# Group norms of SSD and retention: squares and sums on Pool, one ones product per group, retention's heads in two PSUM banks

## The reference

```python
z, xbc, dt_raw, rq, rk, rv, rg = _split(h @ w_in, AB_SIZES)
...
y = (y + xs * d_skip[:, None]).reshape(bsz, l, SSD_D_INNER) * jax.nn.silu(z)
y = group_rms(y, SSD_GROUPS) * ssd_norm
...
r, ret_s = retention_scan(q, k, v, ret_s)
r = jax.nn.silu(rg) * group_rms(r.reshape(bsz, l, RET_V), RET_HEADS)
return jnp.concatenate([y, r], axis=-1) @ w_out, conv_buf, ssm_h, ret_s
```

## Time and profile before

| what | value |
|---|---|
| device time, three runs | 1846.28, 1851.96, 1851.95 us (median 1851.95) |
| the profiled execution: its device time, its span from first to last instruction | 1851.53 us, 1849.6 us |
| busy share of the span: PE, DVE, ACT, POOL | 93%, 68%, 46%, 14% |
| mean granted TensorE clock (share of full speed) | 0.971 |
| the first product of r0, the start of the output projection's matmuls (us from the span's start) | 554.32, 633.96 |

### The profile page before, as it was taken

The page is one execution under the profiler, slowest core; times in us unless marked ns, Lnnn a source line. Parts: engine busy times, 40 slices in busy tenths (PEclk is TensorE's granted clock), DMA queues, the critical chain, the costliest instruction groups (busy, mean ns, idle before and its releaser), DMA issues.

```text
span 1849.6 us, 34017 instructions
## 1 busy us (share of the span) xinstructions
PE 1725.2 (93%) x13610; PEld 1631.4 (88%) x13610; DVE 1255.1 (68%) x2260; ACT 848.8 (46%) x1156; POOL 251.6 (14%) x353
## 2 busy tenths in 40 slices
PE   7999989898997899989999999999997898999998
PEld 7999989887885689887999999999886787799997
DVE  5765677686676654594677767776656678477764
ACT  5433455364336533333455555445444642344443
POOL 1001100200111112120200121002311122020011
PEclk9999989999999898999999999999999998999999
DMA  8665745445576576686698798889834578578884
GB/s 229 182 171 163 212 133 153 131 122 158 170 241 193 179 249 181 212 290 244 172 254 244 227 258 250 264 249 277 244 98 153 175 241 313 188 205 247 268 272 147
DMA packets 470522, 386.58 MB, mean 209 GB/s; under 512 B 15401, under 2 KB 436549, under 8 KB 470341
## 3 DMA queue, kind: packets, MB, share of 16 engines
q1 hardware_dynamic: 409904, 254.87, 47.4%
q0 software_dynamic: 27200, 97.11, 15.5%
q10 hardware_dynamic: 33280, 32.65, 5.2%
HBM read 346.12 MB, written 38.66 MB: 208 GB/s over the span
## 4 chain that ended last, share of the span: by engine, by line
PE 61%; DVE 18%; ACT 14%; issue 6%; DMA 2%; POOL 0%; ACTq 0%; DVEq 0%; SPq 0%; POOLq 0%
PE psum L264 16%; PE psum L265 16%; PE psum L266 16%; DVE wlo L218 6%; ACT whi L212 5%; DVE kc L2300 2%; ACT late L1819 2%; DVE late L1828 2%; PE psum L596 1%; PE psum L2376 1%; PE psum L485 1%; PE psum L2471 1%; PE psum L831 1%; PE psum L1627 1%; PE psum L2419 1%
## 5 line engine op out<-in xcount | busy, mean ns | idle before, releaser
L218 DVE TENSOR_TENSOR wlo<-raw,whi 128x2048 fp32r<-128x2048 f32 (+2 forms) x261 | 552.9, 2119 | 267.5 <-ACT whi L212 266.8
L264 PE MATMUL psum<-xnh,whi 128*128 128x264 f32 x2328 | 675.3, 290 | 12.3 <-DVE ht L851 6.9
L265 PE MATMUL psum<-xnl,whi 128*128 128x264 f32 x2328 | 666.5, 286 | 0.0
L266 PE MATMUL psum<-xnh,wlo 128*128 128x264 f32 x2328 | 665.5, 286 | 0.0
L212 ACT ACTIVATE whi<-raw 128x2048 fp32r<-128x2048 f32 (+2 forms) x261 | 460.8, 1767 | 116.9 <-DMA raw<-in_w_xkv 45.6
L264 PEld LDWEIGHTS psum<-xnh,whi 128*128 128x128 f32 x2328 | 445.8, 191 | 26.2 <-issue 25.2
L265 PEld LDWEIGHTS psum<-xnl,whi 128*128 128x128 f32 x2328 | 445.9, 192 | 1.1
L266 PEld LDWEIGHTS psum<-xnh,wlo 128*128 128x128 f32 x2328 | 443.4, 190 | 0.0
L264 PE MATMUL psum<-Hh,whi 128*128 128x264 f32 x704 | 201.6, 286 | 1.6 <-DVE late L1828 1.6
L266 PE MATMUL psum<-Hh,wlo 128*128 128x264 f32 x704 | 200.6, 285 | 0.0
L265 PE MATMUL psum<-Hl,whi 128*128 128x264 f32 x704 | 200.3, 285 | 0.0
(11 more groups left out here) (589 smaller groups left out, 2906.7 us busy)
## 6 DMA issues: line engine op xcount, KB each, us to landing
raw<-in_w_ffn_in SPq DMA_DIRECT2D x176, 512.0 KB, 5.2
raw<-in_w_in_ab SPq DMA_DIRECT2D x88, 512.0 KB, 4.7
raw<-in_w_ffn_out SPq DMA_DIRECT2D x64, 384.0 KB, 4.6
out<-late ACTq DMA_DIRECT2D x48, 512.0 KB, 5.2
raw<-in_w_ffn_out SPq DMA_DIRECT2D x64, 320.0 KB, 3.5
sb<-in_state_ret POOLq DMA_DIRECT2D x32, 512.0 KB, 5.1
raw<-in_w_out_ab SPq DMA_DIRECT2D x32, 512.0 KB, 5.1
kc<-in_cache_mem_k POOLq DMA_DIRECT2D x32, 512.0 KB, 6.4
```

Source lines behind the costliest of these rows:

```text
L218: nc.vector.tensor_tensor(wlo[:, c % SLOTS, 0:m], raw[:, c % SLOTS, 0:m], whi[:, c % SLOTS, 0:m].bitcast(F32), ALU.subtract).then_inc(lo_d ...
L264: e.matmul(out, a, hi[:, kk, 0:S.cols], start=first, stop=False)
L265: e.matmul(out, a, lo[:, kk, 0:S.cols], start=False, stop=False)
L266: m = e.matmul(out, b, hi[:, kk, 0:S.cols], start=False, stop=final)
```

## The change

Pool squares the four tiles of a group and adds them up in the place where the group's root will stand (`Squares`); PE then runs one ones product for the group (`SumRoot`), followed by the same root and reciprocal. The statistics r0, y0, r1, y1 and so on are taken in this order. Pool's squares are put between its loads of retention states; the gate's multiplication that overwrites a tile of `vf` waits for the group's squares. The SSD groups' applications move: y2 from the hooks of chunk 5 to those of chunk 6, y3 from chunk 6 to chunk 7. Even and odd heads of the sample retention use banks 5 and 7, so a head waits for the copy of the head before the last.

```diff
+        class Squares(Stage):
...
+            def pool(S, e):
+                if S.before:
+                    S.before(e)
+                acc = S.out[:, 0, 0:S.n]
+                for t in range(S.g):
+                    v = S.src[:, t, 0:S.n]
+                    link(e, "pool", e.tensor_tensor(sq[:, t % 2, 0:S.n] if t else acc, v, v, ALU.mult))
+                    if t:
+                        ins = e.tensor_tensor(acc, acc, sq[:, t % 2, 0:S.n], ALU.add)
+                        if t < S.g - 1:
+                            link(e, "pool", ins)
+                ins.then_inc(sq_ready, 1)
+
+        class SumRoot(Stage):
...
+            def pe(S, e):
+                if S.q.g0 > 0:
+                    e.wait_ge(sd_done, S.q.g0)
+                e.wait_ge(sq_ready, S.q.q0 + 1)
+                e.matmul(psum[:, SSB, 0:S.q.n], ones[:, :], S.q.out[:, 0, 0:S.q.n], start=True, stop=True).then_inc(ss_done, 1)
+
+            def act(S, e):
+                e.wait_ge(ss_done, S.q.q0 + 1)
+                nc.scalar.activation(S.q.out[:, 0, 0:S.q.n], psum[:, SSB, 0:S.q.n], ACT.Sqrt, scale=1.0 / (S.q.g * P), bias=eps).then_inc(sd_done, 1)
...
-            part_of = lambda h: slice((h % 2) * 256, (h % 2) * 256 + 256)
+            bank_of = lambda h: 5 + 2 * (h % 2)
...
-                        if h >= 1:
-                            e.wait_ge(rr_copied, h)
+                        if h >= 2:
+                            e.wait_ge(rr_copied, h - 1)
...
                 def mul(e, l, par):
+                    if squares and l % 2 == 0:
+                        e.wait_ge(sq_ready, squares[l // 2].q0 + 1)
...
-            ahead[1] = [BankFour()] + r_stat(0)
-            ahead[2] = y_stat(0)
-            hook[2] = []
-            ret_at[6].extend(r_stat(1))
-            ahead[3] = y_stat(1)
+            for G in range(4):
+                r_sq.append(r_squares(G))
+                y_sq.append(y_squares(G))
+            for G, (cr, cy) in enumerate(((1, 2), (4, 6), (8, 10), (11, 12))):
+                ret_at[cr].insert(0, r_sq[G])
+                ret_at[cy].append(y_sq[G])
+            ahead[1] = [BankFour(), SumRoot(r_sq[0])]
+            hook[2] = [SumRoot(y_sq[0])]
+            ahead[3] = [SumRoot(r_sq[1])]
             hook[3] = y_apply(0)
-            ahead[4] = y_stat(2)
+            ahead[4] = [SumRoot(y_sq[1])]
             hook[4] = y_apply(1)
-            ret_at[10].extend(r_stat(2))
-            ahead[5] = y_stat(3)
-            hook[5] = y_apply(2)
-            hook[6] = y_apply(3)
+            ahead[5] = [SumRoot(r_sq[2])]
+            hook[5] = [SumRoot(y_sq[2])]
+            hook[6] = y_apply(2) + [SumRoot(r_sq[3]), SumRoot(y_sq[3])]
+            y_last = y_apply(3)
             y_split = xn_wait()
-            ahead[7] = r_stat(3)
-            hook[7] = [g_last]
+            hook[7] = y_last + [g_last]
```

More of the change, by code:

```diff
@@ L491, in dve, with __init__ @@
                     e.reciprocal(S.out[:, G, 0:S.n], S.out[:, G, 0:S.n]).then_inc(rstd_done, 1)
+        class Squares(Stage):
+            def __init__(S, src, g, out, before=None, n=T):
+                S.src, S.g, S.out, S.before, S.n = src, g, out, before, n
+                S.q0, S.g0 = tot["sq"], tot["grp"]
+                tot["sq"] += 1
+                tot["grp"] += 1
+            def pool(S, e):
[11 more added lines that the diff above has]
+        class SumRoot(Stage):
+            def __init__(S, squares):
+                S.q = squares
+            def pe(S, e):
[6 more added lines that the diff above has]
+                nc.scalar.activation(S.q.out[:, 0, 0:S.q.n], psum[:, SSB, 0:S.q.n], ACT.Sqrt, scale=1.0 / (S.q.g * P), bias=eps).then_inc(sd_done, 1)
+            def dve(S, e):
+                e.wait_ge(sd_done, S.q.g0 + 1)
+                e.reciprocal(S.q.out[:, 0, 0:S.q.n], S.q.out[:, 0, 0:S.q.n]).then_inc(rstd_done, 1)
         class Apply(Stage):
@@ L1688, in dve @@
                     link(e, "dve", e.tensor_copy(qkb[:, :, :], psum[:, 5, QC:QC + 32].rearrange("p (h b) -> p h b", h=RH)))
-                    e.memset(psum[:, 5, :], 0.0).then_inc(qk_made, 1)
+                    e.wait_ge(ro_out, 2 * RH)
+                    e.memset(psum[:, 5:8:2, 0:256], 0.0).then_inc(qk_made, 1)
                     e.wait_ge(qk_made, 3)
@@ L1722, in pe @@
                         for half in range(2):
-                            m = e.matmul(psum[lane(d, half), 5, part_of(h)], qm[:, h % 2, d, b * NS:(b + 1) * NS], sb[buf(i)][:, d, half * 256:half * 256 + 256],
+                            m = e.matmul(psum[lane(d, half), bank_of(h), 0:256], qm[:, h % 2, d, b * NS:(b + 1) * NS], sb[buf(i)][:, d, half * 256:half * 256 + 256],
                                          start=b == 0, stop=b == NS - 1)
@@ L1931, in mixer_ab, with gated_late @@
             y = xbc[:, 0:16, :]
-            def gated_late(dst, stash, q0, final, ready=None):
+            def gated_late(dst, stash, q0, final, ready=None, squares=None):
                 def act(e, l, par, use):
@@ L2014, in mixer_ab @@
             tot["gate"] += 8
-            ag, dg, g_last = gated_late(vf, gs, qg, 8, ready=at_least(ro_out, 2 * RH))
+            r_sq, y_sq = [], []
+            ag, dg, g_last = gated_late(vf, gs, qg, 8, ready=at_least(ro_out, 2 * RH), squares=r_sq)
             rss = place("rss", [P, RH, NS], at=R2 + 38272)
@@ L2028, in dve @@
                     e.wait_ge(s_used, NS * (h + 1))
-                    e.tensor_scalar(rrow[0:104, h, 0:256], psum[0:104, 5, part_of(h)], gam[h], None, ALU.mult).then_inc(rr_copied, 1)
+                    e.tensor_scalar(rrow[0:104, h, 0:256], psum[0:104, bank_of(h), 0:256], gam[h], None, ALU.mult).then_inc(rr_copied, 1)
                     if h + 2 < RH:
@@ L2089, in mixer_ab, with y_squares, r_squares @@
             t4 = lambda G: slice(4 * G, 4 * G + 4)
-            def y_stat(G):
-                first = lambda e, t: (e.wait_ge(ssd_out, 1), e.wait_ge(y_gated, 1), [e.wait_ge(q, 64) for q in rS_stored]) if t == 0 else None
-                return behind(lambda: Stat(xbc[:, t4(G), :], 1, 4, rstd4[:, G:G + 1, :], first if G == 0 else None))
+            def y_squares(G):
+                first = lambda e: (e.wait_ge(ssd_out, 1), e.wait_ge(y_gated, 1), [e.wait_ge(q, 64) for q in rS_stored]) and None
+                return Squares(xbc[:, t4(G), :], 4, rstd4[:, G:G + 1, :], first if G == 0 else None)
             def y_apply(G):
-                return behind(lambda: Apply(xbc[:, t4(G), :], 1, 4, rstd4[:, G:G + 1, :], G_SSD + 4 * G, yh[:, t4(G), :], yl[:, t4(G), :]))
-            def r_stat(G):
-                return behind(lambda: Stat(vf[:, t4(G), :], 1, 4, rstd_r[:, G:G + 1, :], lambda e, t: (e.wait_ge(ro_out, 2 * G + 2), e.wait_ge(hy_done, 16 * NS)) if t == 0 else None, n=NP))
+                return behind(lambda: Apply(xbc[:, t4(G), :], 1, 4, rstd4[:, G:G + 1, :], G_SSD + 4 * G, yh[:, t4(G), :], yl[:, t4(G), :],
+                                            groups_done=y_sq[G].g0 + 1))
+            def r_squares(G):
+                first = all_of(at_least(ro_out, 2 * RH), at_least(ra_ready, RH), at_least(hy_done, 16 * NS))
+                return Squares(vf[:, t4(G), :], 4, rstd_r[:, G:G + 1, :], first if G == 0 else None, n=NP)
             def r_apply(G):
                 stored_h = at_least(hy_done, 16 * NS) if G == 0 else None
-                return behind(lambda: Apply(vf[:, t4(G), :], 1, 4, rstd_r[:, G:G + 1, :], None, rh_[:, t4(G), :], rl_[:, t4(G), :], n=NP, wait=stored_h))
+                return behind(lambda: Apply(vf[:, t4(G), :], 1, 4, rstd_r[:, G:G + 1, :], None, rh_[:, t4(G), :], rl_[:, t4(G), :], n=NP, wait=stored_h,
+                                            groups_done=r_sq[G].g0 + 1))
             ret_at = [[] for _ in range(33)]
```

## The result

Over 20 executions each, the kernel before takes 1853.72 us (median) and the changed one 1856.38; the ratio is 1.0022, 95% interval 1.0012 to 1.0032. That is 2.2 to 5.9 us more, or 4.1 (0.22%) by the ratio itself; forecast were 2.8 us more (1854).

What follows compares the result with a forecast made beforehand. PE was taken to be bound by its products and by waits in a chain between PE, ACT and DVE. Removing 34.1 us and adding 36.9 gave +2.8 on 1851.5, so 1854 us, range 1846 to 1861.

Steps and rivals of the forecast that it cites:

- What the change removes: PE loses 24 of 32 products, waits for squares and at heads 1 and 2, and slow work: 34.1 us.
- The four waits: New PE waits at r0, y2, y3 and the output projection: 29.55 us, with 7.3 of slow work 36.9 added.
- r0's sum ends: Pool finishes r0's squares and sums at 561.5, with 2.2 us lost beside DVE's split of a chunk.
- wait for r0: PE waits 7.2 us for Pool's sum ahead of r0's product; without any blocking 5.0.
- wait for y2: PE waits 8.85 us ahead of y2's product for r2's root, because of the single bank; 5.65 without blocking.
- wait for y3: PE waits 8.4 us ahead of y3's product for r3's root; without blocking 6.8.
- wait of the output projection: Its first matmul waits 5.1 us for y3's tiles, which now follow the eviction of chunk 7.
- slow work behind the four: PE runs slow behind each new wait, 1.8 us each, 7.3 us with the unrounded mean.
- The price of a meeting: A DVE operation with two SBUF tiles loses 0.30 us beside Pool; two thirds meet, 1.6 us a round.
- rival 1: Blocking decides: all 24 DVE operations of three rounds meet Pool at 0.45 us, +6.0 us, 1860.3; chance 0.24.
- Rivals 2 (no blocking): Pool and DVE do not block each other here: 7.0 us less, 1847.3; chance 0.16.
- Rivals 3 and 4: 3: waits at y2, y3 vanish, 1833.3, chance 0.06; 4: two banks bring nothing in the output projection, 1857.9, chance 0.08.

Runs made afterwards that it cites:

- two_banks: The kernel before with only the change's two PSUM banks, squares and products as they were: 1849.03 us, 0.9984 to the kernel before.
- one_bank: The changed kernel with all heads of the sample retention in one bank again: 1859.91 us, 1.0042 to the kernel before.
- one_square: The changed kernel with Pool squaring only one of four tiles for r1 to y3: 1849.48 us, 0.9980 to the kernel before.
- own_bank: The changed kernel with the sums of r in a PSUM bank of their own: 1848.12 us, 0.9981 to the kernel before.
- act_r0: The changed kernel with r's sums in their own bank, y3's tiles before chunk 7's eviction, r0's squares on ACT with four products: 1840.22 us, 0.9929 to before.
- r0_later: The changed kernel with r0's product, root and reciprocal one chunk later: 1856.32 us, 1.0013 to the kernel before.
- y3_earlier: The changed kernel with the rounding of y3's tiles ahead of chunk 7's eviction: 1850.19 us, 0.9983 to the kernel before.

## Why the prediction was right, point by point

**What the change removes.** All of it went, as the order of time above shows. PE's busy time in the stretch fell from 69.1 to 59.6 us although there is more slow work in it. From head 2's first item to the next it is 3.67 us (653.40 to 657.07), without idle time; 5.09 before, and the 2.17 ahead of it are gone. That the second bank is the cause holds in the order of before (two_banks), while in the changed order the wait had shrunk to 0.43 without it (one_bank). The sum is right, the credit was partly given to the wrong edit.

**The four waits.** The same load that begins Pool's work stands 1.74 us later in this profile (555.12 for the earlier trace rows).

| term | forecast, us | measured, us |
|---|---|---|
| r0's sum ends (less the 1.74) | 561.5 | 561.3 |
| wait for r0 | 7.2 | 6.81 |
| wait for y2 | 8.85 | 9.71 |
| wait for y3 | 8.4 | 7.86 |
| wait of the output projection | 5.1 | 5.21 |
| slow work behind the four | 7.3 | 7.8 |
| added | 36.9 | 37.4 |

Slow work is worked out as before: 569.36 - 563.23 for a product, an item and a half chunk, 6.13 where 4.21 would do (1.9); 612.72 - 607.02, a product and a half chunk, 5.70 for 3.66 (2.0); 5.07 for 3.66 behind y3 (1.4); 5.58 for 3.11 behind the output projection's wait (2.5). The granted clock is a mixture in the first three stretches; in the last it is 0.50, the lower of the two levels (1.2 GHz) from end to end.

**Pool's sums beside DVE's split.** Pool in order of time, at r0 and in the round of y0:

```profile
557.25 2.85 POOL L510 TENSOR_TENSOR rstd_r<-rstd_r,sq 128x256 f32<-128x256 f32 x1
...
562.36 0.72 POOL L510 TENSOR_TENSOR rstd_r<-rstd_r,sq 128x256 f32<-128x256 f32 x1
...
587.35 0.83 POOL L508 TENSOR_TENSOR rstd_r<-vf 128x256 f32<-128x256 f32 x1
588.25 0.69 POOL L508 TENSOR_TENSOR sq<-vf 128x256 f32<-128x256 f32 x1
589.02 0.80 POOL L510 TENSOR_TENSOR rstd_r<-rstd_r,sq 128x256 f32<-128x256 f32 x1
589.90 0.69 POOL L508 TENSOR_TENSOR sq<-vf 128x256 f32<-128x256 f32 x1
```

One operation of r0 is 2.85 us long, beside DVE's split of 2.28: 2.13 over its like, 2.2 forecast. That is the whole of the second part of r0's wait.

**The price of a meeting: right in sum, wrong in its parts.** DVE in order of time:

```profile
557.24 2.28 DVE L218 TENSOR_TENSOR wlo<-raw,whi 128x2048 fp32r<-128x2048 f32 x1
...
584.05 1.21 DVE L1990 TENSOR_TENSOR vf<-vf,ht 128x512 f32<-128x512 f32 x1
...
586.87 0.84 DVE L561 TENSOR_TENSOR yl<-xt,yh 128x264 fp32r<-128x264 f32 x1
587.63 0.84 DVE L556 SCALAR_TENSOR_TENSOR xt<-xbc,g,rstd 128x264 f32<-128x264 f32 x1
588.39 0.84 DVE L561 TENSOR_TENSOR yl<-xt,yh 128x264 fp32r<-128x264 f32 x1
589.15 0.96 DVE L556 SCALAR_TENSOR_TENSOR xt<-xbc,g,rstd 128x264 f32<-128x264 f32 x1
...
595.13 1.79 DVE L533 RECIPROCAL rstd<-rstd 128x264 f32<-128x264 f32 x1
596.84 0.64 DVE L1999 TENSOR_TENSOR ht<-psum,rstd 128x528 f32<-128x528 f32 x1
...
637.46 0.43 DVE L561 TENSOR_TENSOR yl<-xt,yh 128x264 fp32r<-128x264 f32 x1 [0.92 <-ACT yh L584]
```

An application that meets Pool takes 0.84 us where one in y3's round, with Pool idle, takes 0.43: 0.41 more (0.36 for L556), well over my 0.30 and near the 0.45 of rival 1. The gate's multiplication pays 0.53 in that round (1.21 us for 0.68). By single operations rival 1 was closer. What it had wrong is that this adds up on the path: part of the lengthening falls into time in which DVE would have waited for ACT's cast, y2's round meets Pool only in its first half, and so the two waits lost 4.8 us to it (one_square: 3.8 at y2, and 0.9 of the 1.6 at y3). 4.8 over 24 operations is 0.20, which is my 0.30 for two thirds of them. That these errors of mine cancel, in the price of one operation, in how much of it lies on the path and between y2 and y3, is luck. Rivals 2 (no blocking) and 1 are both refuted by one_square, the first by 4.8 us and the second by 6.0; of rival 1 the single price stays.

The DVE rows also tell where there is no price: the reciprocal and the eviction, each with one SBUF input, are as short as in the earlier trace rows in the same dense stretch of Pool's operations (1.79 and 0.64). The Trainium skill ("SBUF — State Buffer", section "Who interferes with whom") says that a VectorE instruction with at most one SBUF input, outside the 2-port perf modes, does not contend with GpSimd, and that one with two contends with a GpSimd instruction that reads SBUF; the ports they share are an exclusive lock, and the second to issue is blocked until the first is through. These rows agree on who meets whom: 2.85 and 0.84 us with two inputs against 1.79 and 0.64 with one. Taken word for word for the time (rival 1) it gave 6.0 us too much, because not every blocked instruction is on the path.

**Rivals 3 and 4.** The waits at y2 and y3 did not vanish (17.6 us), so the plain gain is refuted. Weights or states did not take the place of head 2's wait: from 653.40 to 657.07 PE never stands.

**What the prediction left out.** At 655 us the shift is +4.9, less the 1.9 ahead of the change +3.0, where the sum gave +2.8. From there to the end of the output projection the changed kernel gains another 1.9 us (a shift of +3.0 at 748). About 0.5 is a wait of 0.40 before, at 671.77, that is not there now. The rest lies around the last tail, where PE waits for `rl`. Before, PE runs at a granted clock of 0.78 ahead of that wait (700.00 to 703.48) and of 0.50 behind it (705.86 to 711.00); after, at 1.00 ahead (703.5 to 706.3) and at 0.66 behind (710 to 715). That gives back 1.55 us ahead of the wait and 1.1 behind it, and the wait itself is 1.3 longer (3.70 for 2.38). In the other kernels' profiles the same stretch gives from 3.1 us gained to 0.3 lost. No experiment followed this up, and why PE is slow ahead of the wait in the profile before stays open. So this pair of profiles gives +1.1 in the place where the terms give +2.8. Why the timed runs give 4.1 is not shown; their interval (2.2 to 5.9) holds the forecast, and 20 executions of the kernel before scatter from 1846.28 to 1857.49 us, more than the three differ.

## What to carry to other kernels

Before crediting an edit with a wait that it removes, follow the waiting engine to its next wait in the new order: here 34 us of waits and work went and 37 came back, at four places that could all be computed beforehand from rows of the old profile. Moving reductions to an idle engine pays only as far as that engine keeps ahead: once the single bank is out of the way, PE waits 6 to 7 us each for Pool's sums of y2 and y3, with eight groups on Pool (own_bank) as with seven (act_r0). With seven groups, a second bank for the sums and y3's tiles in another place, the same idea is 13 us faster than the kernel before all the same. Test a wait by moving it a little later: if it turns up again at the next product (r0_later, 6.0 for 6.8 us), its cause is elsewhere; if it is gone (y3_earlier), it was only order.

## What the runs showed of the hardware that was not expected

- In a dense stretch of both, Pool and DVE take turns, one by one. From 586.87 to 589.90 us they start at 586.87 (DVE), 587.35 (Pool), 587.63, 588.25, 588.39, 589.02, 589.15, 589.90: never two of one engine in a row. DVE's applications come 0.76 us apart, where they follow each other in 0.35 to 0.40 us with Pool idle (one_square, from 586.00 on). DVE's operations double in length, Pool's squares grow from 0.61 to 0.69 us.
- Beside a long DVE operation it is the reverse: one Pool operation takes 2.5 to 2.9 us, and DVE's split stays at 2.28 to 2.29 in all but two cases (2.43 and 2.79).
- Behind each of the four waits PE was slow, at a granted clock of 0.50 to 0.69, and lost 1.4 to 2.5 us of work; the loss did not grow with the wait (the shortest, 5.21 us, cost the most, 2.5).
